# One core, four mixer and MLP layers in float32: the first stage's load order and passes, the layer boundaries and the softmax layers' order of work

## The reference

```python
def first_block(...):                       # DEPTH = 2
    c_act = silu(c)
    for i in range(DEPTH):
        sh1, sc1, g1, sh2, sc2, g2 = split(c_act @ w_ada[i] + b_ada[i], 6)
        u = x * (1.0 + sc1) + sh1
        y = gla_mixer(u, ...) if i % 2 == 0 else chunk_attention(u, ...)
        x = layer_norm(ALPHA * x + (1.0 + g1) * y, ...)
        u = x * (1.0 + sc2) + sh2
        y = square(relu(u @ w1)) @ w2
        x = layer_norm(ALPHA * x + (1.0 + g2) * y, ...)
def second_block(...):                      # x from the first block
    for l in range(DEPTH):
        h = rms_norm(x, norm_g[l]) * (1.0 + scale) + shift
        y = even_mixer(h, ...) if l % 2 == 0 else odd_mixer(h, ...)
        x = x + gate * y
```

## Time and profile before

| | |
|---|---|
| median of 3 runs | 1739.59 us (1739.51 to 1740.22) |
| the profiled execution's own time | 1740.15 us |
| its span, first to last instruction | 1738.4 us |
| mean granted TensorE clock | 1.000 |
| busy share of PE, DVE, ACT, POOL | 99%, 60%, 44%, 47% |
| HBM read | 239.21 MB, 139 GB/s over the span |

### The profile page before, as it was taken

How to read it: one execution, slowest core, us unless ns; L and a number is a source line. 1 busy time by engine, 2 the same in 40 slices (tenths; PEclk the granted TensorE clock), 3 DMA queues, 4 the chain that set the end, 5 groups by cost and what they waited for, 6 DMA issues and landing times.

```text
span 1738.4 us, 24573 instructions
## 1 busy us (share of the span) xinstructions
PE 1714.2 (99%) x9199; PEld 1429.3 (82%) x9199; DVE 1041.7 (60%) x1716; ACT 760.1 (44%) x1329; POOL 809.2 (47%) x616
## 2 busy tenths in 40 slices
PE   8999999999999999999999999999999999999999
PEld 7777788888888788888888888887888888888887
DVE  5877567555564963663475555678387844237652
ACT  4443644222223354653532222234544556667650
POOL 6535337555555463232465555553533335453342
PEclk9999999999999999999999999999999999999999
DMA  9635237444444233222274444442222223334422
GB/s 375 238 133 199 94 108 266 169 169 169 169 168 159 97 133 111 85 97 74 79 285 169 169 169 169 169 166 76 97 73 67 71 77 98 104 96 133 139 90 73
DMA packets 114829, 242.65 MB, mean 140 GB/s; under 512 B 6144, under 2 KB 27776, under 8 KB 114736
## 3 DMA queue, kind: packets, MB, share of 16 engines
q1 hardware_dynamic: 112560, 237.20, 39.3%
q10 hardware_dynamic: 2176, 4.19, 0.7%
HBM read 239.21 MB, written 2.16 MB: 139 GB/s over the span
## 4 chain that ended last, share of the span: by engine, by line
PE 91%; DMA 3%; DVE 3%; ACT 1%; POOL 1%; issue 1%; SPq 0%; POOLq 0%; DVEq 0%; ACTq 0%
PE bank L238 43%; PE bank L641 20%; PE bank L1596 5%; PE bank L1562 4%; PE bank L440 3%; PE bank L1564 2%; PE bank L420 2%; PE bank L1674 2%; PE bank L1662 2%; PE bank L1638 1%; DMA ct<-cumd 1%; PE bank L2160 1%; PE bank L404 1%; DMA x<-in_x 1%; POOL wsp L2655 1%
## 5 line engine op out<-in xcount | busy, mean ns | idle before, releaser
L2655 POOL TENSOR_TENSOR wsp<-raw,wsp 128x512 fp32r<-128x512 f32 x520 | 770.4, 1514 | 826.6 <-ACT wsp L193 826.6
L238 PE MATMUL bank<-xT,wsp 128*128 128x512 f32 x2088 | 482.7, 390 | 1.6 <-POOL wsp L2659 0.9
L238 PEld LDWEIGHTS bank<-xT,wsp 128*128 128x128 f32 x2088 | 390.9, 188 | 85.2 <-POOL wsp L2659 1.3
L193 ACT ACTIVATE wsp<-raw 128x1024 fp32r<-128x1024 f32 x132 | 139.8, 1059 | 477.4 <-PE bank L641 248.0
L641 PE MATMUL bank<-wsp,hT 128*128 128x512 f32 x1344 | 315.9, 395 | 0.0
L641 PEld LDWEIGHTS bank<-wsp,hT 128*128 128x128 f32 x1344 | 253.2, 188 | 59.0
L238 PE MATMUL bank<-wsp,xT 128*128 128x512 f32 x1248 | 297.9, 394 | 0.6 <-DVE xT L508 0.4
L238 PEld LDWEIGHTS bank<-wsp,xT 128*128 128x128 f32 x1248 | 230.7, 188 | 53.3 <-issue 5.7
L854 DVE CUSTOM_DVE_ANT_0 ada_ring<-ada_ring,crow,cols 128x1024 f32<-128x1024 f32 x96 | 150.7, 1605 | 5.1 <-DMA ada_ring<-in_ada_rows 5.1
L196 ACT ACTIVATE wsp<-raw 128x1024 fp32r<-128x1024 f32 x132 | 138.3, 1048 | 0.0
L775 DVE TENSOR_TENSOR x<-bank,x 128x512 f32<-128x512 f32 x80 | 55.2, 690 | 115.9 <-PE bank L641 115.9
(11 more groups left out here) (328 smaller groups left out, 2176.3 us busy)
## 6 DMA issues: line engine op xcount, KB each, us to landing
raw<-in_ff_w SPq DMA_DIRECT2D x64, 1024.0 KB, 5.2
ada_ring<-in_ada_rows SPq DMA_DIRECT2D x96, 512.0 KB, 6.1
tok<-in_ada_rows SPq DMA_DIRECT2D x32, 512.0 KB, 5.0
raw<-in_odd_w_in SPq DMA_DIRECT2D x16, 1024.0 KB, 5.5
raw<-in_gla_w_in SPq DMA_DIRECT2D x12, 1024.0 KB, 6.8
raw<-in_att_w_in SPq DMA_DIRECT2D x12, 1024.0 KB, 5.3
raw<-in_even_w_in SPq DMA_DIRECT2D x12, 1024.0 KB, 5.2
ring_s<-in_ada_rows SPq DMA_DIRECT2D x16, 512.0 KB, 10.5
```

The costliest lines, as they stand in the source:

```text
L193: act.activation(wsp[:, slot, 0, 0:HK // 2], raw[:, slot, 0:HK // 2], ACT.Copy).then_inc(hi_part, 1)
L238: mm = pe.matmul(out_ap, l, r, start=(start and a == b), stop=(stop and a == 1))
L2655: ins = pool.tensor_tensor(wsp[:, slot, 1, k], raw[:, slot, k], wsp[:, slot, 0, k].bitcast(F32), ALU.subtract)
```

## The change

1. First stage, SP: the second weight half is issued behind group 1's columns. For groups 2 and 3 the columns go ahead of the tiles.
2. First stage, PE: 3 + 3 + 2 of the unread matmuls. The products wait for the high part, and for a low part only at the second pass. For feature tiles 2 and 3, 4 and 5, 6 and 7 the high and weight-low passes of both come first, then the transposes of the next group, then the activation-low passes of both; the last pair's go by token tile. POOL makes the four weight low parts of the second half before the two of `xT`.
3. Boundaries: group 0's transposes are moved ahead of the last piece, except for `in_even_in`. `pe_first_panel` goes in the order `LAST_COLUMN`, waits for high parts only, and for a weight's low part at the second pass. ACT writes the high part before `u32`. Group 1 is transposed ahead of the second activation-low pass (third in even, fourth in odd). On ACT the root of tile 3 (in odd its sum of squares too) comes after four items. On DVE as many low parts precede tile 3 as passes precede group 1.
4. Softmax layers: `out_ahead(0)` is moved ahead of the last pair's transposes. Where the piece `dense(u + 2)` is of two feature tiles it is moved ahead of the fourth unit's transposes (pairs 0 and 2 of att, pairs 0, 2, 4 and 6 of odd).
5. SP waits for the strips of pair 4 to land before it issues `column_half(5)`. A buffer of 96 floats for each partition that nothing uses is put behind `w16` and moves every buffer allocated after it.

```diff
+        sb("line_pad", [P, 96])
...
@@ pe_panel
+                if (t, h) == (ST - 1, 1) and turn:
+                    turn()
...
@@ pe_first_panel
+        LAST_COLUMN = [(k, t) for k in (0, 1) for t in range(ST - 1)] + [(0, ST - 1), (1, ST - 1)] + [(k, t) for k in (2, 3) for t in range(ST)]
+        TURN_AT = {"in_even_in": 2, "in_odd_in": 3}
-            pe_turned_group(pe, ts, need, 0)
             for g in range(2):
-                for k, t in WAVE:
-                    if t == 0:
-                        low_ready(pe, j, k)
-                        if g:
-                            pe.wait_ge(s["u_made"], s["k0"] + HK + k + 1)
-                        else:
-                            pe.wait_ge(s["bank_free"], k + 1)
+                for k, t in LAST_COLUMN:
+                    if t == 0 and g:
+                        pe.wait_ge(s["u_made"], s["k0"] + HK + k + 1)
+                    elif t == 0:
+                        pe.wait_ge(hi_part if k < HK // 2 else hi_made, j + 1)
+                        pe.wait_ge(s["bank_free"], k + 1)
...
                     for b in range(2):
+                        if b and t == 0 and g == 0:
+                            low_ready(pe, j, k)
...
-                    if g == 0 and k == 2:
-                        pe_turned_group(pe, ts, need, 1)
+                    if g == 0 and k == TURN_AT.get(ts, 1):
+                        pe_turned_group(pe, ts, 1)
...
@@ act_turned
-                if HK <= n < KT:
+                if n < HK:
+                    act.activation(out[:, 0], src, ACT.Identity, **kw).then_inc(s["bank_free"], 1)
+                    act.activation(u, src, ACT.Identity, **kw).then_inc(s["u_made"], 1)
+                elif n < KT:
...
@@ down_pair
+                    if (l, t, q) == (0, ST - 1, 1):
+                        pe_turned_group(pe, "in_att_in", 0)
...
@@ act_normalised_tiles
-            act_turned(act, ts, range(0, 2))
+            act_turned(act, ts, range(0, HK))
             act_root(act, name, 3)
-            act_turned(act, ts, range(2, KT))
+            act_turned(act, ts, range(HK, KT))
...
@@ gla_pe, first stage
+            def first_highs(k):
+                pe.wait_ge(hi_made, k // HK + 1)
+                pe.wait_ge(free, k + 1)
+                for t in range(ST):
+                    for b in range(2):
+                        if t == 0 and b:
+                            low_ready(pe, base["gla_in"] + k // HK, k % HK)
+                        pe.matmul(bank[t][:, :], wsp[:, k // HK, b, k % HK, t * P:t * P + P], xT[:, 0, k, :], ...)
...
+            for k in range(2):
+                first_highs(k)
+                for t in range(ST):
+                    first_low(k, t)
+                if k == 0:
+                    pe_first_x(pe, 1)
+            for g in range(1, HK):
+                first_highs(2 * g)
+                first_highs(2 * g + 1)
+                if g < HK - 1:
+                    pe_first_x(pe, g + 1)
+                    for k in (2 * g, 2 * g + 1):
+                        for t in range(ST):
+                            mm = first_low(k, t)
...
@@ pe_out
+                if (t, h) == (ST - 1, 1) and name == "att_out":
+                    pe_turned_group(pe, "hid_ff1", 0)
...
@@ pe_pairs
-                turned(u)
                 if last and ahead:
                     out_ahead(0)
-                for w in range(u + 1, u + ST):
+                quarters = u + 2 in work and work[u + 2][6] - work[u + 2][5] == KT // ST
+                for w in range(u, u + ST):
+                    if w == u + 3 and quarters:
+                        dense(u + 2)
                     turned(w)
-                dense(u + 2)
+                if not quarters:
+                    dense(u + 2)
...
@@ sync engine
-            for g in range(HK):
+            for g in range(2):
                 first_tiles(g, range(HK))
                 x_columns(g)
-                if g in (0, 2):
-                    first_weights(g // 2)
+                first_weights(g)
+            for g in range(2, HK):
+                x_columns(g)
+                first_tiles(g, range(HK))
...
+            sp.wait_ge(ct_ld, 16 * ST * 5)
             column_half(5)
...
@@ gpsimd
                 low_of(1, k)
-                if k < 2:
-                    split_x(HK + k)
+            for k in range(2):
+                split_x(HK + k)
...
@@ tensor
-            pe_at_work(pe, 10)
+            pe_at_work(pe, 3)
...
-            pe_panels(pe, "gla_out", "mid_gla_out", [("NN", 1)], begin=pe_first_half_gla)
+            pe_panels(pe, "gla_out", "mid_gla_out", [("NN", 1)], begin=pe_first_half_gla, turn=lambda: pe_turned_group(pe, "hid_ff0", 0))
...
+            pe_turned_group(pe, "in_even_in", 0)
...
+                      turn=lambda: pe_turned_group(pe, "in_odd_in", 0))
...
@@ last_tile_and_lows
-                dve_lows(dve, ts, range(0, 2))
+                ahead = TURN_AT.get(ts, 1)
+                dve_lows(dve, ts, range(0, ahead))
                 dve_last_tokens(dve, ts, need, 3)
-                dve_lows(dve, ts, range(2, KT + HK))
+                dve_lows(dve, ts, range(ahead, KT + HK))
```

More of the change, by code:

```diff
@@ L239, in pe_tile, with pe_panel @@
             return mm
-        def pe_panel(pe, j, bk, kind, free, free_at, ts, first, last, between=None, begin=None):
+        def pe_panel(pe, j, bk, kind, free, free_at, ts, first, last, between=None, begin=None, turn=None):
             if first and begin:
@@ L259, in pe_panel, with pe_panels @@
                     mm.then_inc(tile_done, 1)
-        def pe_panels(pe, name, ts, runs, between=None, begin=None):
+        def pe_panels(pe, name, ts, runs, between=None, begin=None, turn=None):
             s = TS[ts]
@@ L268, in pair @@
                         pe_panel(pe, base[name] + 4 * i + 2 * b, 4 * b, kind[b], s["bank_free"], 8 * i + 4 * b, s,
-                                 b == 0 and isinstance(i, int), b == 1 and kind == "NN", between, begin)
+                                 b == 0 and isinstance(i, int), b == 1 and kind == "NN", between, begin, turn if b == 1 else None)
                 if pairs > 1:
@@ L377, in group_at, with pe_turned_group @@
             return bank[ST + 2 * g + k // 2][:, k % 2 * GCOLS:k % 2 * GCOLS + GCOLS]
-        def pe_turned_group(pe, ts, need, g):
+        NEED = {"hid_ff0": 2, "in_att_in": 1, "hid_ff1": 1, "in_even_in": 1, "in_odd_in": 1}
+        def pe_turned_group(pe, ts, g):
             s = TS[ts]
-            pe.wait_ge(s["tok_ready"], need + 2 * g + 1)
+            pe.wait_ge(s["tok_ready"], NEED[ts] + 2 * g + 1)
             for t in range(2 * g, 2 * g + 2):
@@ L395, in pe_turned_rest, with pe_first_panel @@
                 mm.then_inc(s["tr_done"], 1)
-        def pe_first_panel(pe, ts, j, need, sums, done):
+        LAST_COLUMN = [(k, t) for k in (0, 1) for t in range(ST - 1)] + [(0, ST - 1), (1, ST - 1)] + [(k, t) for k in (2, 3) for t in range(ST)]
+        TURN_AT = {"in_even_in": 2, "in_odd_in": 3}
+        def pe_first_panel(pe, ts, j, sums, done):
             s = TS[ts]
@@ L1189, in gla_pe @@
             ts = TS["in_gla_in"]
-            for k in range(KT):
-                low_ready(pe, base["gla_in"] + k // HK, k % HK)
+            def first_highs(k):
+                pe.wait_ge(hi_made, k // HK + 1)
                 pe.wait_ge(free, k + 1)
-                if k < 2:
-                    for a in range(2):
-                        if a:
-                            pe.wait_ge(ts["xT_ready"], ts["k0"] + k + 1)
-                        for t in range(ST):
-                            for b in range(2 - a):
-                                mm = pe.matmul(bank[t][:, :], wsp[:, 0, b, k, t * P:t * P + P], xT[:, a, k, :],
-                                               start=(k == 0 and a == 0 and b == 0), stop=False)
-                for t in range(ST if k >= 2 else 0):
-                    mm = pe_tile(pe, bank[t][:, :], k // HK, k % HK, k, t, "T", k == 0, k == KT - 1,
-                                 (ts["xT_ready"], ts["k0"] + k + 1) if t == 0 else None)
-                    if k == KT - 1 and t < ST - 1:
-                        mm.then_inc(tile_done, 1)
-                if k % HK == HK - 1:
-                    mm.then_inc(w_used, 1)
-                if k % 2 == 0 and k < KT - 2:
-                    pe_first_x(pe, k // 2 + 1)
@@ new lines, in first_highs, with first_low @@
+                for t in range(ST):
+                    for b in range(2):
+                        if t == 0 and b:
+                            low_ready(pe, base["gla_in"] + k // HK, k % HK)
+                        pe.matmul(bank[t][:, :], wsp[:, k // HK, b, k % HK, t * P:t * P + P], xT[:, 0, k, :],
+                                  start=(k == 0 and b == 0), stop=False)
+            def first_low(k, t):
+                if t == 0:
+                    pe.wait_ge(ts["xT_ready"], ts["k0"] + k + 1)
```

(5 more changed lines are left out.)

20 lines of the change are left out of this document (13 added, 7 removed).

## The result

| | before | after |
|---|---|---|
| median, us (range, executions) | 1739.86 (1739.51 to 1740.22, 4) | 1721.75 (1720.58 to 1723.2, 4) |
| profiled execution; its span, us | 1740.15; 1738.4 | 1720.94; 1719.2 |

The ratio is 0.9892, with a 95% interval of 0.9877 to 0.9907. Forecast was 1727.7 us, between 1725.3 and 1731.8.

A forecast was written before the change was run, and what follows sets the result against it. PE, busy for 99% of the span, was taken as the bound, so only its waits could be won: boundaries 9.55, att 1.2, odd 0, first stage 1.1, together 11.9 us, giving 1727.7 us, range 1725.3 to 1731.8.

The forecast's parts named there:

- I take 0, with 1 us to either side.: Whole kernel: address shifts from the unused buffer were forecast to win 0, with 1 us to either side.
- can win only what PE waits: Whole kernel: PE's summed work sets the time, so a change leaving products alone wins only PE's waits.
- 9.55: Layer boundaries: forecast gain in us, summed as 2.25 + 2.1 + 2.2 + 3.0, with 0 at in_even_in.
- So PE runs 3.92 us through: Boundary into hid_ff0: copies arrive in time, so the first panel's two passes run 3.92 us, to 250.7.
- Tile 3, the rival: Layer-norm boundaries: token tile 3's root comes 0.5 us or more late, group 1's transposes stop; 1731.0 us, 17%.
- the chain named: in_even_in: group 1 waits for token tile 3 through an unshortened DVE and ACT chain; gain 0, at most 0.2 us.
- Softmax att: Last pair of att: the moved piece of 12 matmuls covers PE's 1.4 us wait for DVE; 1.2 us won.
- up to 0.75 us: Odd's first stop: gain from the moved quarter, given back at the next pair because of the strips; net 0.
- 1.6 us: First stage: gain from seven unread matmuls fewer, PE starting near 18.0 instead of 19.45.
- 46.19 - 1.6 - 2.0 + 2.3 + 0.1 = 45.0: First stage: its end in us, from 46.19 before; 1.1 us taken as won, ends -0.5 and 2.0.
- the early load pays nothing: First stage rival: queue gap and group 3's later tiles eat the 1.6 us; total 1729.3 us, 12%.
- The clock: First-stage rival: fewer unread matmuls and a longer stop drop PE to 1.2 GHz; 1739.7 or 1752.7 us, 3%.

The follow-up runs named there:

- e2: The kernel before with the unused buffer of 384 bytes per partition alone: 1731.15 us against 1741.09, ratio 0.9941.
- e11: The changed kernel with the first of ScalarE's two high copies of a weight half cut in two: 1719.93 us.
- e3: The kernel before with the boundary changes alone, without buffer, first stage's part or softmax order: 1732.7 us, ratio 0.9949.
- e12: The kernel before with the softmax layers' order and SP's wait for the strips alone: 1740.37 us against 1740.35, ratio 0.9998.
- e10: The changed kernel run once more, nothing altered: 1721.52 us, ratio to the kernel before 0.9882.
- e17: The changed kernel run again in a later comparison, nothing altered: 1723.88 us.
- e13: The kernel before with 400 unused bytes where the change has 384 (next buffer moves by 416), one execution: 1740.93 us.
- e14: The kernel before with 448 unused bytes where the change has 384, one execution: 1742.08 us.
- e15: The kernel before with 64 unused bytes where the change has 384, one execution: 1734.49 us.
- e7: The kernel before with 128 unused bytes ahead of all buffers, one execution: 1738.98 us.
- e8: The kernel before with 128 unused bytes ahead of all buffers and the change's 384 as well, one execution: 1728.54 us.

## Why the prediction was right and wrong

**The unused buffer: the step that failed.** "I take 0, with 1 us to either side." It is 10 us. I priced the shift on one pair of rows in which the same kind of instruction had operands ahead of the buffer and behind it, eight transposes at 1.03 and 1.09 us, and let that bound everything. Even there it was not the address: in e2, with the buffer alone, the transposes of `aP` follow one another at 109.4 ns, where they did at 109.5. The rows that mattered stood beside each other in the trace of before: 96 up products at 21.96 us, 96 down products at 22.48, the same shape on the same engine, with the stationary operand ahead of the buffer in the one and behind it in the other. I read "busy" as work that no reordering can change, and said so ("can win only what PE waits"); for an edit that moves addresses that sentence does not hold. Those rows give 14 x 0.56 = 7.8 us as the upper bound in the down products, and the range would have reached below 1720.

**Boundaries: mechanism right, 8.1 us for 9.55.** 1.74 for 2.25, 1.88 for 2.1, 1.85 for 2.2, -0.09 for 0, 2.74 for 3.0. The term mis-sized is "So PE runs 3.92 us through". I had the weights' low parts rightly at 1.35 us apart, but set the need for the last at 250.2. With PE's products 0.98 us a column, and columns 0 and 1 interleaved, it is needed at some 249.9, 0.2 us ahead of POOL. e11 confirms it: with POOL earlier, the block takes 3.83 us. With e11 the four blocks are shorter, but the layers around them give it back. Tile 3, the rival to which I gave 17%, didn't take over at the three layer-norm boundaries; the transposes of group 1 follow without a stop, so the slack of 0.5 us was there. Even stayed at 0 by the chain named, but not with the stops that I expected: the one for token tile 3 did not grow to 1.1 us, it stayed at 0.62, and PE waits earlier, for 1.03, 0.19 and 0.32 us inside the first panel.

**Softmax att: right.** 1.3 us for 1.2. **Odd: right at 0, but by luck**: the first pair's stop did not give the "up to 0.75 us" that the second pair was to take back. It stayed, and the second pair's stop went, with nothing won. The stops also move by a microsecond from one execution to the next. Two profiles could not have judged this term in either direction.

**First stage: wrong, 0 for 1.1 us.** Two steps failed. "1.6 us" for the unread matmuls: PE then stops for ACT's high part of the weights (0.93 us at 17.52), and its first product comes at 17.56 to 18.95 (seven profiles, mean 18.4) where it came at 18.35 to 20.21 (thirteen profiles, mean 19.4): 1.0 us, not the 1.45 to "near 18.0". And the sum "46.19 - 1.6 - 2.0 + 2.3 + 0.1 = 45.0" carried it through to the end, although the one stop left, for feature tile 4, is set by the loads and takes up what PE has won before it: 34.68 in the changed kernel, where the sum had 32.8 to 33.8. That is the rival "the early load pays nothing", to which I gave 12%.

**The clock**, the rival at 3%, is real, though not as placed. It does not make the change slower, as it falls with the old order as well: 6 of 13 profiles, 4 of 7 with the new. I let it last for the rest of the stage (12 us); it lasts some 3.4 and costs 0.9 to 1.6. The Trainium skill (TensorE: Matmul & The Clock Gate, Part 1: The HAM clock gate) has the half rate come back after idleness. The rows at 0.50 behind the stop agree in ten profiles; in the ten others no such row follows, behind stops of up to 2.46 us.

**The sum.** The parts by themselves are 10.2 us (e2), 8.9 (e3), 1.3 (the trace of e12) and 0, 20.4 together. The changed kernel won 18.1, 18.8 (e10) and 16.2 (e17). The intervals of the ratios are 2 to 3 us to either side, so this is no sign of a loss between the parts, nor does it rule one out.

**Left open.** Whether matmuls on unread data inside that stop would keep the clock up, for the 0.9 to 1.6 us, wasn't tried. Why the products' rate depends on the distance isn't shown, only that it does, and no distances but 0, 32, 64, 128 and 192 were run, 32, 64 and 192 once each.

## What to carry to other kernels

Compare the rate of one kind of product over all its pairs of operands before you look for waits; two rows of equal shape with unequal time are a finding, and an edit that changes the size or order of buffers is to be priced by them. A stop that ends with a transfer takes up whatever the engine won ahead of it. And judge a term of a microsecond by several profiles: single ones differed here by 2 us in the first stage and 1 us in one softmax layer, with no change at either place.

## What the runs showed of the hardware

- The down products, matmuls of 512 fp32r columns, follow one another at 226.7 ns (21.76 us between the starts of rows, by 96) where the stationary operand's start is at distance 0 from the streamed one's modulo 256 bytes, 232.5 at 128, 233.3 at 32 and 64 (22.40 by 96, e13 and e14) and 229.0 at 192 (21.98 by 96, e15). Moving both together by 128 bytes changes nothing (e7, e8).
- PE's granted clock fell to 0.50 for some 3.4 us behind a stop of 2.3 to 2.8 us with the new order, and stayed at 1.00 behind stops of 1.75, 2.09 and 2.46 us in other executions, so the stop's length alone doesn't decide it. With the old order it fell behind 1.7 to 2.8 us and stayed behind 1.6 and less.
- A stop that is shorter than the pipelined end of a block does not show as a wait: the 0.33 us at the boundary into `hid_ff0` (0.3 us at three others) could be read only from the starts.
